# Two transformer blocks on one core: eight FFN up projections by seven block products, with sums of weights on GpSimd

## What is computed

```python
h = _rms(x, norm_g[l, 2]) * (1.0 + scale_f) + shift_f
a, g = jnp.split(h @ ffn_w_in[l], 2, axis=-1)
x = x + (gate_f * _rms((jax.nn.silu(a) * g) @ ffn_w_out[l], norm_g[l, 3])).astype(x.dtype)
```

## Time and profile before

| | |
|---|---|
| time, median of 3 runs | 2585.65 us (2585.51 to 2586.03) |
| profiled execution, span | 2583.7 us |
| its own time | not given apart; median less span is 1.95 us |
| PE busy | 2564.6 us, 99% |
| DVE busy | 2003.3 us, 78% |
| ACT busy | 1369.5 us, 53% |
| POOL busy | 252.5 us, 10% |
| DMA | 611.08 MB, mean 237 GB/s |

### The profile page before, as it was taken

The page is one execution under the profiler, slowest core; times in us unless marked ns, Lnnn a source line. Parts: engine busy times, 40 slices in busy tenths (PEclk is TensorE's granted clock), DMA queues, the critical chain, the costliest instruction groups (busy, mean ns, idle before and its releaser), DMA issues.

```text
span 2583.7 us, 34752 instructions
## 1 busy us (share of the span) xinstructions
PE 2564.6 (99%) x12080; PEld 2129.4 (82%) x12080; DVE 2003.3 (78%) x2580; ACT 1369.5 (53%) x1809; POOL 252.5 (10%) x312
## 2 busy tenths in 40 slices
PE   9999999999999999999999999999999999999998
PEld 8888888888888887888888777888788888888887
DVE  6898788788878889876686888787856666666898
ACT  6545566656665656455556444444644444444444
POOL 0021022223222000080000000000000000000000
PEclk9999999999999999999999999999999999999999
DMA  9667788878787986756555775799566666666785
GB/s 319 227 216 253 228 278 265 282 256 309 255 288 252 318 275 211 265 172 224 174 178 168 254 242 195 247 313 319 175 205 194 192 192 194 193 191 192 259 299 191
DMA packets 278364, 611.08 MB, mean 237 GB/s; under 512 B 19916, under 2 KB 21136, under 8 KB 276336
## 3 DMA queue, kind: packets, MB, share of 16 engines
q1 hardware_dynamic: 273696, 583.53, 69.2%
q0 software_dynamic: 4416, 26.13, 2.8%
q10 hardware_dynamic: 144, 0.01, 0.0%
HBM read 599.08 MB, written 11.29 MB: 236 GB/s over the span
## 4 chain that ended last, share of the span: by engine, by line
PE 92%; DVE 4%; ACT 1%; DMA 1%; issue 1%; SPq 0%; DVEq 0%; ACTq 0%
PE ps L670 92%; DMA w_raw<-in_w_in 1%; DVE w_lo L2111 1%; DVE arena L2106 1%; ACT w_hi L1338 1%; PE ps L807 0%; DVE arena L3104 0%; DMA w_raw<-in_ffn_w_out 0%; PE ps L828 0%; DVE arena L2132 0%; DVE x L2132 0%; ACT arena L1379 0%; PE ps L1254 0%; DVE x L2106 0%; DVE mod_parts L2254 0%
## 5 line engine op out<-in xcount | busy, mean ns | idle before, releaser
L1338 ACT ACTIVATE w_hi<-w_raw 128x1024 fp32r<-128x1024 f32 (+1 forms) x898 | 948.3, 1057 | 1135.5 <-PE ps L670 1037.4
L2111 DVE TENSOR_TENSOR w_lo<-w_raw,w_hi 128x1024 fp32r<-128x1024 f32 x809 | 1001.3, 1240 | 473.0 <-ACT w_hi L1338 468.8
L670 PE MATMUL ps<-w_hi,hop_part 128*128 128x512 f32 x4264 | 1334.2, 391 | 3.2 <-DVE w_lo L2111 2.0
L670 PEld LDWEIGHTS ps<-w_hi,hop_part 128*128 128x128 f32 x4264 | 800.3, 188 | 176.4 <-issue 5.1
L670 PE MATMUL ps<-w_lo,hop_part 128*128 128x512 f32 x2132 | 829.6, 389 | 0.0
L670 PEld LDWEIGHTS ps<-w_lo,hop_part 128*128 128x128 f32 x2132 | 400.3, 188 | 81.5
L670 PE MATMUL ps<-w_hi,hid_hi_part 128*128 128x512 f32 x992 | 387.1, 390 | 0.0
L670 PE MATMUL ps<-w_lo,hid_hi_part 128*128 128x512 f32 x992 | 386.0, 389 | 0.0
L670 PE MATMUL ps<-w_hi,hid_lo_part 128*128 128x512 f32 x992 | 386.0, 389 | 0.0
L2106 DVE SCALAR_TENSOR_TENSOR arena<-arena,cs 128x768 f32<-128x768 f32 x240 | 245.9, 1025 | 0.3
L670 PE MATMUL ps<-hop_part,w_hi 128*128 128x512 f32 (+1 forms) x992 | 236.1, 380 | 2.0 <-ACT w_hi L1338 1.1
(11 more groups left out here) (335 smaller groups left out, 1352.5 us busy)
## 6 DMA issues: line engine op xcount, KB each, us to landing
arena<-in_ada_w SPq DMA_DIRECT2D x256, 384.0 KB, 5.2
w_raw<-in_ffn_w_in SPq DMA_DIRECT2D x176, 512.0 KB, 4.4
w_raw<-in_w_up SPq DMA_DIRECT2D x128, 512.0 KB, 4.3
w_raw<-in_w_down SPq DMA_DIRECT2D x128, 512.0 KB, 4.9
w_raw<-in_w_gate SPq DMA_DIRECT2D x128, 512.0 KB, 4.4
w_raw<-in_ffn_w_out SPq DMA_DIRECT2D x88, 512.0 KB, 4.5
w_raw<-in_w_out SPq DMA_DIRECT2D x64, 512.0 KB, 5.3
w_raw<-in_wide_columns SPq DMA_DIRECT2D x64, 512.0 KB, 4.1
```

The source lines that it names most:

```text
L670: return nc.tensor.matmul(o, w, r, start=start, stop=stop, skip_group_check=True)
L1338: return nc.scalar.activation(o, i, ACT.Copy, scale=scale)
L2111: V.tensor_tensor(w_lo[:, j % LEAD, :, 0:cols], w_raw[:, j % RAW, :, 0:cols], w_hi[:, j % LEAD, :, 0:cols].bitcast(F32), ALU.subtract).the ...
```

## The change

The eight blocks of the loop are written as 64 **steps** (GROUPS), without a loop. For each of the eight column blocks the up projections of a and g together, [h1 h2] by [w11 w12; w21 w22] in 2x2 blocks (two token tiles by a and g, two k-tiles), are done by a form with seven block products in place of eight. The products are named in SEVEN; four use sums of activations (`s_forms`, made once by POOL, split by ACT and DVE), and four use sums of weights.

One step g takes one k pair of both a and g (two DMAs of 512 KB, `load_pair`). POOL makes the sums of weights with three TENSOR_TENSOR (128x1024, 128x512, 128x512; named A, B and C in the prediction). ACT and DVE split seven pieces in four instructions each (`form_hi`, `form_lo`, F0 to F3: three of 128x1024, one of 128x512). PE runs 21 matmuls into seven PSUM banks (`group`) and then one down **visit**, one 512-column chunk of one token tile, 12 matmuls, for the group three steps earlier (`visit`). The down weights are split in `down_hi` and `down_lo` (128x1024, once a step), and `drain` adds the visit to `ACC_TOK`. The freed SBUF comes from x, parked in HBM by a POOL DMA of 2 MB and fetched back after the loop.

At the end of each column block (`end_step`, `end_sum`, `end_first`, `end_silu`) the seven banks are joined by five DVE additions (one input in PSUM), two ACT copies, two ACT Silus and four POOL operations of 128x512. The product is turned by eight PE transposes in two goes, in place of the 16 STREAM_TRANSPOSE.

```diff
+SEVEN = ("11", "12", "s2", "s4", "s1", "s3", "22")
+SEVEN_BANK = (4, 5, 6, 0, 1, 2, 3)
+SUPERS = FFN_SUPER - 3
+GROUPS = SUPERS * UA
+VISITS = GROUPS
+SHIFT = 3
...
+        for s in range(GROUPS):
+            if s < 2:
+                sp.wait_ge(sem["lo_ready"], R_FFN * 8 + 15 + s)
+            else:
+                sp.wait_ge(sem["down_lo"], HEADS + s - 1)
+            load_down(s)
+            if s + 3 < GROUPS:
+                sp.wait_ge(sem["lo_ready"], forms(s + 2))
+                load_pair(s + 3)
...
+        def group(g):
+            c, i = g // UA, g % UA
+            for p, name in enumerate(SEVEN):
+                if p % 2 == 0:
+                    pe.wait_ge(sem["lo_ready"], forms(g, p // 2 + 1))
+                if i == 0:
+                    bank_free(c, p)
+                mm(o, left(name, i, 0), wh, start=i == 0, stop=False)
+                mm(o, left(name, i, 0), wl, start=False, stop=False)
+                m = mm(o, left(name, i, 1), wh, start=False, stop=i == UA - 1)
+                if p % 2 or p == len(SEVEN) - 1:
+                    m.then_inc(sem["unit_done"], 1)
+                if p == 1 and i in (1, 2):
+                    turn_product(c, i - 1)
...
+        for s in range(GROUPS + SHIFT):
+            if s < GROUPS:
+                group(s)
+            if s >= SHIFT:
+                visit(s - SHIFT, s)
...
+        def form_hi(g, i):
+            act.wait_ge(sem["unit_done"], forms(g - 1, i + 1))
+            if i == 0:
+                act.wait_ge(pair_in[g % 2], 16 + 32 * (g // 2 + 1))
+            else:
+                act.wait_ge(sem["sums_made"], HEADS + 4 + 3 * g + FORM_SUMS[i])
+            copy(piece(w_hi, FORM_AT[i], FORM_N[i]), form_raw(g, i)).then_inc(sem["hi_ready"], 1)
...
+        def form_lo(g, i):
+            dve.wait_ge(sem["hi_ready"], forms(g, i + 1))
+            V.tensor_tensor(piece(w_lo, FORM_AT[i], FORM_N[i]), form_raw(g, i), piece(w_hi, FORM_AT[i], FORM_N[i]).bitcast(F32),
+                            ALU.subtract).then_inc(sem["lo_ready"], 1)
...
+        for s in range(-1, GROUPS + SHIFT + 1):
+            if s > SHIFT:
+                drain(s - SHIFT - 1)
+            if 0 <= s - 2 < VISITS:
+                down_lo(s - 2)
+            end = super_end(s)
+            if end is not None:
+                end_step(end, 0)
+            next_lo(s, 0)
+            if s % UA in (1, 2) and 0 < s < GROUPS:
+                up_lo(s // UA, s % UA - 1)
+            if end is not None:
+                end_step(end, 1)
+            next_lo(s, 1)
+            if end is not None:
+                end_step(end, 2)
+            next_lo(s, 2)
+            if end is not None:
+                end_step(end, 3)
+            next_lo(s, 3)
+            if end is not None:
+                end_step(end, 4)
...
+        pool.dma_start(x_scratch[:], x[:]).then_inc(sem["x_parked"], 16)
+        act_sum(0, rows[:, :, 0, 1], rows[:, :, 1, 1], ALU.add)
...
+        for g in range(GROUPS + 1):
+            end = after_end(g - 1)
+            if g < GROUPS:
+                raw, sums_at = PAIR_RAW[g % 2], t_sums(g)
+                pool.wait_ge(pair_in[g % 2], 16 + 32 * (g // 2 + 1))
+                G.tensor_tensor(sums_at, raw[:, 1], raw[:, :, 0], ALU.subtract).then_inc(sem["sums_made"], 1)
+                pool.wait_ge(sem["sums_made"], HEADS + 4 + 3 * g + 1)
+                G.tensor_tensor(raw[:, 1, 0], raw[:, 1, 1], sums_at[:, 0], ALU.subtract).then_inc(sem["sums_made"], 1)
+            if end is not None:
+                end_sum(end, 2)
+            if g < GROUPS:
+                pool.wait_ge(sem["lo_ready"], forms(g, 1))
+                G.tensor_tensor(raw[:, 0, 1], raw[:, 0, 1], raw[:, 1, 0], ALU.subtract).then_inc(sem["sums_made"], 1)
+            if end is not None:
+                end_sum(end, 3)
+            if g % UA == 0 and 0 < g:
+                end_sum(g // UA - 1, 0)
+                end_sum(g // UA - 1, 1)
+        pool.wait_ge(sem["visit_used"], HEADS + 2 * VISITS)
+        pool.dma_start(x[:], x_scratch[:]).then_inc(sem["x_back"], 16)
```

More of the change, by code:

```diff
@@ L635, in _ @@
             load(R_FFN, q, w_ffn_in[q % UA, :, :, col:col + COLS])
[L636 to L645, removed]
@@ new lines, in _ @@
+        sp.wait_ge(sem["lo_ready"], R_FFN * 8 + 14)
+        load_pair(0)
+        sp.wait_ge(sem["hop_ready"], HOP[7] + KT + 4)
+        load_pair(1)
+        sp.wait_ge(sem["lo_ready"], forms(1))
+        load_pair(2)
+        for s in range(GROUPS):
[7 more added lines that the diff above has]
+                load_pair(s + 3)
@@ L1310, in ffn_step, with bank_free @@
             down(R, at + 16, H + 1, 0, par, m + (base + 1), between=between)
[L1312 to L1316, removed]
+        def bank_free(c, p):
+            if c == 0:
+                if p >= 3:
+                    pe.wait_ge(drained[0 if p < 5 else 1], H_FFN + 2)
+            else:
+                read = (("end_act", 4, 1), ("end_dve", 5, 1), ("end_dve", 5, 2), ("end_dve", 5, 4), ("end_act", 4, 3),
+                        ("end_dve", 5, 3), ("end_dve", 5, 5))[p]
+                pe.wait_ge(sem[read[0]], HEADS + read[1] * (c - 1) + read[2])
@@ new lines, in turn_product @@
+        def turn_product(c, t):
+            if c == 0:
+                pe.wait_ge(drained[1], H_FFN + 2)
+            else:
+                pe.wait_ge(sem["end_pool"], 4 * (c - 1) + 3 + t)
+            if UA * c + 1 + t > SHIFT:
+                pe.wait_ge(sem["visit_drained"], HEADS + UA * c + 1 + t - SHIFT)
+            if t == 1:
+                pe.wait_ge(sem["hid_ready"], base + 2 * c + 1)
+            for f in range(FT):
+                m = nc.tensor.transpose(PS[VISIT_BANK][:, f * P:(f + 1) * P], PROD_TOK[:, t, f * P:(f + 1) * P], ident)
+            m.then_inc(sem["hid_turned"], 1)
@@ L2073, in _ @@
         for j in range(UA - LEAD):
-            split(R + 6, j + LEAD)
+            split(R + 6, j + LEAD, skip=R_LATE - R_FORM)
         for c in range(2):
@@ new lines, in up_lo, with drain @@
+        def up_lo(c, t):
+            dve.wait_ge(sem["hid_hi"], MLP_SUPER + 2 * c + t + 1)
+            cols = slice(t * P, (t + 1) * P)
+            V.tensor_tensor(hid_lo[:, c % 2, :, cols], PS[VISIT_BANK][:].rearrange("p (f n) -> p f n", f=FT),
+                            hid_hi[:, c % 2, :, cols].bitcast(F32), ALU.subtract).then_inc(sem["hid_ready"], 1)
+        def drain(v):
+            d, n, t = visit_of(v)
+            bank = SPARE_BANK if v - (VISITS - SHIFT) in (0, 2) else VISIT_BANK
+            dve.wait_ge(sem["visit_used"], HEADS + 2 * v + 2)
+            V.tensor_tensor(ACC_TOK[:, t, part(n)], PS[bank][:], ACC_TOK[:, t, part(n)], ALU.add).then_inc(sem["visit_drained"], 1)
@@ L3114, in _ @@
+        for j in range(2 * UA - LEAD):
             split(R_FFN, j + LEAD)
```

260 lines of the change are left out of this document (217 added, 43 removed).

## The result

The changed kernel takes **2753.53 us** in the median of four runs (2751.6 to 2755.36), against 2585.58 for the kernel before on the same chip: ratio 1.0648, 95% interval 1.0633 to 1.0663. It is 6.5% slower. Predicted were 2739 us, with 2675 to 2845 as the range. The profiled execution has a span of 2751.2 us, 167.5 more than before.

A forecast was written before the change was run, and what follows sets the result against it. PE bounds the kernel before; afterwards turns of DVE and POOL do. The span of 2583.7 plus 140.6 for eight blocks and 13 for edges gives 2737.3; with 1.95 for the median, 2739 us, range 2675 to 2845.

The forecast's parts named there:

- What bounds the kernel now: In the loop before the change PE is always busy and sets the end, at 65.1 us a block.
- How DVE and POOL share: DVE instructions with two SBUF inputs and POOL instructions reading SBUF take turns, whole instructions at a time, in issue order.
- The step: In each loop step the turns of DVE and POOL sum to 9.52 us, against 8.14 before and PE's 7.5.
- A's term: POOL's 1024-element sum of weights in each step: 1.99 at least plus 0.11 to change over, 2.10 us.
- The drain is free: In each step DVE's drain, with one PSUM input, runs beside a POOL sum and costs nothing; otherwise 0.60 us.
- The loads are hidden: The pair of weight DMAs for each step lands about 1 us or more early, so it costs nothing.
- Column block ends: Once per eight steps, POOL's four operations, uncovered DVE additions and the `up_lo` halves add 6.5 us, between 4.2 and 9.
- Edges: Before and after the loop, last visits, the first group's wait and x's return add 13 us, between 6 and 22.
- the return of x: Fetching x back under the late part after the loop costs 1 us, from nothing to 7.6.
- Rival 1 (overlap): In the loop splits and sums overlap after all, PE stays the bound: 2562 us; 4%, 5% with its neighbour.
- Rival 2 (a longer chain): Waits among four engines in the loop lose 1.5 to 2 us a step, 10 an end: about 2885 us; 11%.
- Rival 3 (the clock): PE's idling in the loop brings its clock to 1.2 GHz, 14.9 us a step, about 3030 us; 3%.

The follow-up runs named there:

- the lighter PE: The changed kernel with the last of each product's three matmuls left out, 7 of 33 matmuls a step: 2755.02 us, ratio 1.0656.

## Why the prediction was right, point by point

- **What bounds the kernel now.** Right. PE sets the end before, and with the sums away the step falls to PE's own 7.5 us.
- **How DVE and POOL share.** Right, and shown: the pairs of the earlier trace rows are the pattern of the whole loop. Writes are exempt, a single read input of POOL is not, and PE has no part in it.
- **The step.** 9.52 predicted, 9.53 measured. F2, B, C and L are within 0.02 us. A's turn took 2.26 and not 2.10; F3 took 0.55 and not 0.60, F0 and F1 took 2.28 and not 2.34. That these misses cancel is luck: alone, A's would be 0.16 x 64 = 10 us. The working of A's term was wrong too: it added 0.11 for changing over to the least time alone. The shortest A of the loop takes 2.40, as both in the earlier trace rows did, and an addition of 512 elements takes 1.26 alone in the loop (at 2573.44), so a queued one's turn is 0.1 us shorter than its time alone and not longer. The 1.99 and 1.04 are of other tiles; why those are quicker wasn't isolated.
- **The drain is free.** Right in the common step, wrong in two of a block's eight steps. The prediction itself said that a drain costs its 0.60 where the order puts B elsewhere, and then counted such places only in its upper bound.
- **The loads are hidden.** Nearly: 5 us.
- **Column block ends, 6.5 us.** Mis-sized: 7.7, by the two drains with no turn of POOL beside them, 2 x 0.6 = 1.2 us. Without drains a block is 82.6, eight steps of 9.53 and 6.3. 8 x 1.2 = 10 us; the eight cost 150 more than before, where I had 140.6.
- **Edges, 13 us.** Mis-sized: 17.5, the rest of 167.9. One piece is PE's wait of 10.2 us ahead of the last two visits. The trace names its cause, the late part's first weight load, at 2563.35, and the place of its split in DVE's order; I had cost this at nothing. It isn't the return of x, on which I had put 1 us: that is issued at 2587.45, when the wait is over. How much a different order there would give back wasn't tried. These two terms, 10 and 4.5 us, make up the distance from 2739 to 2753.5.
- **Rival 1 (overlap)** is out, since the sums and the splits take turns in the loop, and its time would be wrong even so: with no sums at all the form took 2592 us and not 2562, since block ends take back 4 us each and the edges 12.
- **Rival 2 (a longer chain)** appeared only in the ends and at the last edge; DVE has an instruction in it for 97% of the middle, where this rival had it idle a fifth of the time.
- **Rival 3 (the clock).** The granted clock fell to 0.94 in the loop, where I had forecast 1.00 from the earlier trace rows. In the common steps the forecast held, PE's short gaps left the clock at 1.00; around the block ends, where PE idled for 2.7 to 4.8 us, it came down to a mix of both levels:

```profile
2028.00:2058.00 30.00, 27.10 (x113) 20.28 (x112) 30.00 (x21) 14.98 (x17) 21.86 (x10) 1.00 0.48 160
2144.00:2180.00 36.00, 25.23 (x94) 18.87 (x93) 34.67 (x25) 15.84 (x19) 28.18 (x14) 0.86 0.41 132
```

After the 10.2 us wait, a pair of matmuls takes 1.05 at 2580.01, where a like pair takes 0.63 at 2584.67: the 1.2 GHz level and then the 2.4 GHz one. It set no time in the loop, as the lighter PE shows: PE has 2 us of slack in a step. I had given a cost to this case only as a whole and not as a part.

Why none of the placements tried helps: DVE alone needs 8.33 us a step and PE had 8.14 before, so with everything on DVE the eight blocks are 12 us longer by their steps, 66 by their ends, and 11 by the edges. The ends are 8.2 us each: five additions and two `up_lo` halves at 0.6, four sums at about 0.65, and waits. And even the sums for nothing (2592 us) leave the form 6 us behind. Had the 12 us of edges gone too, it would be 2580 by estimate, 0.2% ahead. Neither a repair of the edges nor another place for the two bare drains was tried, nor were any of the sums put on ACT, which is busy for 190 of 400 us.

## What to carry to other kernels

Before work goes to an idle GpSimd, put its SBUF-reading instructions and Vector's instructions with two SBUF inputs into one queue and add up their turns; if that sum passes the time of the engine that bounds the kernel, the move loses, and the same work on Vector may well be the shorter queue (70 us here). Lay what has an input in PSUM beside GpSimd's turns, and look at every such place and not at a typical one: here two of eight had no cover, and this cover goes when a turn is moved. A form that saves 8% of matmuls must also pay for its joins: count the ends of its blocks and the edges before the sums.

## What the hardware showed that I had not expected

- GpSimd's MEMSET left Vector's splits at 1223 ns while GpSimd was busy 60% of the time (1271 on average for those from `arena`, which take 1288 with no MEMSET at all); a plain COPY, with one input, raised them to 1464 and 1605 ns on average.
- A turn of GpSimd costs 1.15 us for 512 elements if it was already queued behind Vector's instruction, and 1.37 if it was released by it. With nothing beside it such an addition takes 1.26 in the loop and 1.04 in the earlier trace rows; what makes this difference wasn't isolated.
- A window of common steps kept the granted clock at 1.00 with PE busy for 27.1 of 30 us; idle stretches of PE of 2.7 to 4.8 us at the block ends went with 0.86 there and 0.94 over the loop. With a third of the up projection's matmuls left out it was 0.89.
